# Last product of a SwiGLU feed-forward part and its layer norm: features on the partitions, or tokens

## The reference

```python
D_FF = -(-8 * D_MODEL // (3 * 256)) * 256      # 2816
def layer_norm(x, g, b):
    mu = jnp.mean(xf, axis=-1, keepdims=True)
    var = jnp.mean(jnp.square(xf - mu), axis=-1, keepdims=True)
    y = (xf - mu) * lax.rsqrt(var + LN_EPS)
    return (y * g.astype(jnp.float32) + b.astype(jnp.float32)).astype(x.dtype)
...
x = layer_norm(alpha * x + mix, ln1_g[l], ln1_b[l])
ff = swiglu_ffn(x, w_ffn_gate[l], w_ffn_up[l], w_ffn_down[l])   # (silu(x Wg) * (x Wu)) Wd
x = layer_norm(alpha * x + ff, ln2_g[l], ln2_b[l])
```

## Time and profile before

| | |
|---|---|
| median of 3 runs | 955.96 us (953.98 to 956.77) |
| the profiled execution's own time | 955.32 us |
| its span, first to last instruction | 953.5 us |
| TensorE busy | 889.1 us, 93% |
| VectorE busy | 626.1 us, 66% |
| ScalarE busy | 430.0 us, 45% |
| mean granted TensorE clock | 0.974 |
| DMA over the span | mean 142 GB/s |

### The profile page before, as it was taken

One profiled execution on the slowest core, in us unless ns is written; L12 is line 12 of the kernel. 1 busy time (PEld: TensorE's weight loads), 2 busy tenths in 40 slices (PEclk: granted clock), 3 DMA queues, 4 the chain that ended last, 5 costly groups with the idle time before them and its releaser, 6 DMA issues.

```text
span 953.5 us, 14351 instructions
## 1 busy us (share of the span) xinstructions
PE 889.1 (93%) x5858; PEld 743.8 (78%) x5858; DVE 626.1 (66%) x1242; ACT 430.0 (45%) x721; POOL 0.2 (0%) x4
## 2 busy tenths in 40 slices
PE   4899999999997999999999999898998899999994
PEld 1567468766686958667988888888887899999993
DVE  4442848565657489466699989875685755555554
ACT  3252426444533463455444444564644644444432
POOL 0000000000000000000000000000000000000000
PEclk9899999999997999999999999899999999999998
DMA  9674542101222312433665555331544355557531
GB/s 346 248 287 171 199 177 78 44 2 53 81 89 60 123 60 74 177 102 132 210 198 172 194 177 177 113 100 54 177 129 136 125 184 179 177 161 216 169 98 44
DMA packets 40722, 135.71 MB, mean 142 GB/s; under 512 B 4432, under 2 KB 5584, under 8 KB 40528
## 3 DMA queue, kind: packets, MB, share of 16 engines
q1 hardware_dynamic: 39792, 130.48, 40.8%
q10 hardware_dynamic: 864, 4.32, 1.2%
HBM read 133.73 MB, written 1.05 MB: 141 GB/s over the span
## 4 chain that ended last, share of the span: by engine, by line
PE 81%; DVE 12%; ACT 4%; DMA 1%; issue 1%; SPq 0%; ACTq 0%; DVEq 0%
PE ps L359 12%; PE ps L360 12%; PE ps L364 10%; PE ps L429 3%; PE ps L431 3%; PE ps L430 3%; PE ps L461 3%; PE ps L697 2%; DVE wlo L1384 2%; PE ps L387 2%; PE ps L720 2%; PE ps L606 2%; PE ps L362 2%; DVE AF L1855 1%; PE ps L388 1%; PE ps L389 1%
## 5 line engine op out<-in xcount | busy, mean ns | idle before, releaser
L359 PE MATMUL ps<-hh,whi 128*128 128x256 f32 (+1 forms) x912 | 267.4, 293 | 3.7 <-DVE AF L1900 2.6
L1384 DVE TENSOR_TENSOR wlo<-raw,whi 128x1024 fp32r<-128x1024 f32 (+3 forms) x206 | 233.8, 1149 | 52.8 <-ACT whi L932 52.7
L360 PE MATMUL ps<-hl,whi 128*128 128x256 f32 (+1 forms) x912 | 263.7, 289 | 0.0
L932 ACT ACTIVATE whi<-raw 128x1024 fp32r<-128x1024 f32 (+3 forms) x206 | 204.5, 997 | 128.3 <-DMA raw<-wpack 49.1
L364 PE MATMUL ps<-hh,wlo 128*128 128x256 f32 (+1 forms) x792 | 229.1, 289 | 0.0
L359 PEld LDWEIGHTS ps<-hh,whi 128*128 128x128 f32 x912 | 176.2, 193 | 9.1 <-issue 5.3
L360 PEld LDWEIGHTS ps<-hl,whi 128*128 128x128 f32 x912 | 176.4, 193 | 2.3 <-issue 0.7
L364 PEld LDWEIGHTS ps<-hh,wlo 128*128 128x128 f32 x792 | 153.3, 194 | 1.4
L429 PE MATMUL ps<-whi,hh 128*128 128x512 f32 (+1 forms) x192 | 70.8, 369 | 0.8 <-ACT wk L1035 0.8
L430 PE MATMUL ps<-wlo,hh 128*128 128x512 f32 (+1 forms) x192 | 70.2, 366 | 0.0
L431 PE MATMUL ps<-whi,hl 128*128 128x512 f32 (+1 forms) x192 | 70.2, 366 | 0.0
(11 more groups left out here) (254 smaller groups left out, 1456.3 us busy)
## 6 DMA issues: line engine op xcount, KB each, us to landing
raw<-wpack SPq DMA_DIRECT2D x172, 512.0 KB, 4.1
AF<-wmod SPq DMA_DIRECT2D x40, 512.0 KB, 6.1
raw<-wpack SPq DMA_DIRECT2D x16, 448.0 KB, 3.9
raw<-wpack SPq DMA_DIRECT2D x24, 256.0 KB, 3.3
XT<-xin SPq DMA_DIRECT2D x4, 512.0 KB, 6.7
raw<-wpack SPq DMA_DIRECT2D x4, 432.0 KB, 5.2
uq<-wuq ACTq DMA_DIRECT2D x2, 768.0 KB, 5.7
cst<-cpack ACTq DMA_DIRECT2D x1, 1093.0 KB, 7.9
```

The source lines that it names most:

```text
L359: e.matmul(o, wh[:, b], xh(k), start=j == 0, stop=False, skip_group_check=True)
L360: e.matmul(o, wh[:, b], xl(k), start=False, stop=False, skip_group_check=True)
L932: e.activation(W.hi(i), W.raw(i), ACT.Copy).then_inc(*HI.up(j))
L1384: e.tensor_tensor(W.lo(i), W.raw(i), W.hi(i), ALU.subtract).then_inc(*LO.up(j))
```

## The change

The down product now has the 128 tokens of one tile t as its output partitions and 1024 output features along the free axis, in two PSUM banks for each t, so four banks are held from f = 0 to f = 21. Its stationary operand is a 128 by 128 block of fh or fl, its moving operand 512 columns of a row block of w_down, and one chunk of weights is the whole row block f (128 by 1024). For one f and one t there are six matmuls (three products by two halves of the features). The down step of f - 3 stands behind the gate and up products of f, for f up to 20. The last four f (18 to 21, from `LAST`) stand at the end, first all four for tokens 0 to 127, then all four for tokens 128 to 255; their chunks are given back after the second pass.

In the first four turns four transposes each bring x (the residual) to tokens on the partitions, and ScalarE scales them by alpha into x3t. The norm is done for one tile of tokens at a time on the free axis: one VectorE instruction adds PSUM and x3t and sums the row; ScalarE squares with bias minus mean and sums; VectorE multiplies by gain in the meantime, makes the root on 128 by 1 elements, and writes the result in two halves of 512 columns. SyncE writes four pieces of 256 KB. Gain and bias of the last norm arrive as rows repeated on all partitions, 1 MB, in a DMA that ScalarE issues behind the weights of w_o.

```diff
+LAST = KF - 4
...
+    def down(f, ts):
+
+        if 0 in ts:
+            down_w[f] = weights(("fd", f), ("w_ffn_down_2", 0, (f,), (0, D)), D)
+        c, wh, wl = down_w[f]
+        pe.wait_ge(V["f", f])
+        for t in ts:
+            if f == 0:
+                pe.wait_ge(*ps.take(("fd", t), 2, hold=True))
+            x = slice(t * P, (t + 1) * P)
+            for y, w in ((K.fh, wh), (K.fh, wl), (K.fl, wh)):
+                for q in range(2):
+                    i = e.matmul(ps.ap(("fd", t), 512, 512 * q), y[:, f % 8, x], w[:, 512 * q:512 * q + 512], ...)
+            i.then_inc(*M.up(("fd", f, t)))
+        if 1 in ts:
+            W.given[c] = M.now()
...
-        for m in range(KD):
-            lin(("fd", f0, m), "w_ffn_down_2", 0, (P * m, P), range(f0, f0 + nf), lambda k: K.fh[:, k - f0, :], lambda k: K.fl[:, k - f0, :], 256, lambda k: V["f", k])
-    ln_sums("ln2")
+        if f < 4:
+            t, q = f // 2, f % 2
+            pe.wait_ge(A["x3", 4 * q + 3], *ps.take(("x3t", f)))
+            for j in range(4):
+                i = e.transpose(ps.ap(("x3t", f), P, j * P), K.XT[:, 4 * q + j, 256 + t * P:384 + t * P], C("ident"))
+            i.then_inc(*M.up(("x3t", f)))
+        if 3 <= f < LAST + 3:
+            down(f - 3, (0, 1))
+    for t in range(2):
+        for f in range(LAST, KF):
+            down(f, (t,))
...
+    e.dma_start(K.AF[:, 3072:5120], K.l2rows).then_inc(*K.l2_in.up("rows"))
...
-            ac.wait_ge(V["fu", m], M["fd", f0 - PARTS[0][1] if f0 == 8 else 8, 7] if f0 else None)
+        ac.wait_ge(V["fu", m], M["fd", m - 8, 1] if m >= 8 else None)
...
+        if m < 4:
+            t, q = m // 2, m % 2
+            ac.wait_ge(M["x3t", m])
+            e.activation(g.x3t[:, t, 512 * q:512 * q + 512], ps.ap(("x3t", m)), ACT.Copy, scale=ALPHA).then_inc(*A.up(("x3t", m)))
...
+    for t in range(2):
+        ac.wait_ge(V["lnm", t])
+        e.activation(K.AF[:, 9216:10240], g.x3t[:, t, :], ACT.Square, bias=K.nrm[:, 6 * t:6 * t + 1], accum_out=K.nrm[:, 6 * t + 1:6 * t + 2]).then_inc(*A.up(("lnv", t)))
...
+    for t in range(2):
+        nm, v, u, w = (K.nrm[:, 6 * t + i:6 * t + i + 1] for i in (0, 1, 2, 3))
+        x, y = g.x3t[:, t, :], g.yt[:, t, :]
+        dv.wait_ge(M["fd", KF - 1, t], A["x3t", 2 * t + 1])
+        e.tensor_tensor_reduce(x, ps.ap(("fd", t), D), x, 1.0, 0.0, ALU.add, ALU.add, nm).then_inc(*V.up())
+        dv.wait_ge(V.now())
+        e.tensor_scalar(nm, nm, -1.0 / D, None, ALU.mult, ALU.bypass).then_inc(*V.up(("lnm", t)))
+        dv.wait_ge(V.now(), K.l2_in["rows"])
+        e.scalar_tensor_tensor(out=y, in0=x, scalar=nm, in1=g.l2g, op0=ALU.add, op1=ALU.mult).then_inc(*V.up())
+        dv.wait_ge(A["lnv", t])
+        e.tensor_scalar(v, v, 1.0 / D, LN_EPS, ALU.mult, ALU.add).then_inc(*V.up())
+        rsqrt(v, u, w)
+        dv.wait_ge(V.now())
+        for q in range(2):
+            c = slice(512 * q, 512 * q + 512)
+            e.scalar_tensor_tensor(out=y[:, c], in0=y[:, c], scalar=v, in1=g.l2b[:, c], op0=ALU.mult, op1=ALU.add).then_inc(*V.up(("y", t, q)))
...
-    for k in range(KD):
-        sp.wait_ge(K.act["y", k])
-        e.dma_start(outs[:, k, :], K.XT[:, k, XC]).then_inc(*K.s_out.up("out"))
+    for t in range(2):
+        for q in range(2):
+            sp.wait_ge(K.dve["y", t, q])
+            e.dma_start(K.out[t * P:(t + 1) * P, 512 * q:512 * q + 512], K.G[2].yt[:, t, 512 * q:512 * q + 512]).then_inc(*K.s_out.up("out"))
```

More of the change, by code:

```diff
@@ L905, in tensor_program @@
     xt3 = lambda k: V["x3", k]
[L906 to L914, removed]
-        for m in range(KD):
-            lin(("fd", f0, m), "w_ffn_down_2", 0, (P * m, P), range(f0, f0 + nf), lambda k: K.fh[:, k - f0, :], lambda k: K.fl[:, k - f0, :], 256, lambda k: V["f", k])
-    ln_sums("ln2")
+    def down(f, ts):
[9 more added lines that the diff above has]
+                for q in range(2):
+                    i = e.matmul(ps.ap(("fd", t), 512, 512 * q), y[:, f % 8, x], w[:, 512 * q:512 * q + 512], start=f == 0 and y is K.fh and w is wh, stop=f == KF - 1 and y is K.fl, skip_group_check=True)
+            i.then_inc(*M.up(("fd", f, t)))
+        if 1 in ts:
+            W.given[c] = M.now()
+    down_w = {}
+    for f in range(KF):
+        cc = (P * f, P)
+        if f == 0:
+            lin_many([(("up" if w == "w_ffn_up_2" else "fg", f), w, 0, cc, x2h, x2l, 256) for w in ("w_ffn_gate_2", "w_ffn_up_2")], xt3)
+        else:
+            lin(("fg", f), "w_ffn_gate_2", 0, cc, range(KD), x2h, x2l, 256, xt3)
+            lin(("up", f), "w_ffn_up_2", 0, cc, range(KD), x2h, x2l, 256, xt3)
+        if f < 4:
[9 more added lines that the diff above has]
+            down(f, (t,))
 def scalar_program(K, e):
@@ L1353, in scalar_program @@
     x3(KD - 1)
[L1354 to L1361, removed]
-            ac.wait_ge(V["fu", m], M["fd", f0 - PARTS[0][1] if f0 == 8 else 8, 7] if f0 else None)
[L1363 to L1366, removed]
-    for k in range(KD):
-        ac.wait_ge(V["y", k])
-        e.activation(XT[:, k, XC], XT[:, k, XC], ACT.Identity, bias=C("l2b", k, 1)).then_inc(*A.up(("y", k)))
+    for m in range(KF):
+        z = m % 2 * 256
+        highs(("fg", m))
+        ac.wait_ge(M["fg", m], V["fu", m - 2] if m >= 2 else None)
+        e.activation(K.AF[:, z:z + 256], ps.ap(("fg", m), 256), ACT.Silu).then_inc(*A.up(("fg", m)))
+        ps.give(("fg", m), A.now())
+        highs(("up", m))
+        ac.wait_ge(V["fu", m], M["fd", m - 8, 1] if m >= 8 else None)
+        e.activation(K.fh[:, m % 8, :], K.AF[:, 512 + z:768 + z], ACT.Copy).then_inc(*A.up(("f", m)))
+        if m < 4:
+            t, q = m // 2, m % 2
+            ac.wait_ge(M["x3t", m])
+            e.activation(g.x3t[:, t, 512 * q:512 * q + 512], ps.ap(("x3t", m)), ACT.Copy, scale=ALPHA).then_inc(*A.up(("x3t", m)))
+            ps.give(("x3t", m), A.now())
+        if 3 <= m < LAST + 3:
+            highs(("fd", m - 3))
+    highs(("fd", LAST))
+    for t in range(2):
+        ac.wait_ge(V["lnm", t])
+        e.activation(K.AF[:, 9216:10240], g.x3t[:, t, :], ACT.Square, bias=K.nrm[:, 6 * t:6 * t + 1], accum_out=K.nrm[:, 6 * t + 1:6 * t + 2]).then_inc(*A.up(("lnv", t)))
 def vector_program(K, e):
@@ L2018, in vector_program @@
     x3_low(KD - 1)
[L2019 to L2041, removed]
+    for m in range(KF):
+        z = m % 2 * 256
+        lows(("fg", m))
+        lows(("up", m))
+        h = K.AF[:, 512 + z:768 + z]
+        dv.wait_ge(M["up", m], A["fg", m], V["f", m - 2] if m >= 2 else None)
+        e.tensor_tensor(h, K.AF[:, z:z + 256], ps.ap(("up", m), 256), ALU.mult).then_inc(*V.up(("fu", m)))
+        ps.give(("up", m), V.now())
+        dv.wait_ge(A["f", m])
+        e.tensor_tensor(K.fl[:, m % 8, :], h, K.fh[:, m % 8, :], ALU.subtract).then_inc(*V.up(("f", m)))
+        if 3 <= m < LAST + 3:
+            lows(("fd", m - 3))
@@ L2088, in sync_program, with build @@
     chunks(19, len(W.plan))
-    outs = K.out.rearrange("(k p) n -> p k n", p=P)
-    for k in range(KD):
-        sp.wait_ge(K.act["y", k])
-        e.dma_start(outs[:, k, :], K.XT[:, k, XC]).then_inc(*K.s_out.up("out"))
+    for t in range(2):
+        for q in range(2):
+            sp.wait_ge(K.dve["y", t, q])
+            e.dma_start(K.out[t * P:(t + 1) * P, 512 * q:512 * q + 512], K.G[2].yt[:, t, 512 * q:512 * q + 512]).then_inc(*K.s_out.up("out"))
     sp.wait_ge(K.s_out["out"])
-def build(nc, cpack, xin, wpack, wmod, wuq, wukv, out):
+def build(nc, cpack, xin, wpack, wmod, wuq, wukv, l2rows, out):
     with ExitStack() as ctx:
@@ L2104, in sig @@
             return Sig(ctx.enter_context(nc.semaphore(name)), step)
-        K.cpack, K.xin, K.wpack, K.wmod, K.wuq, K.wukv, K.out = cpack, xin, wpack, wmod, wuq, wukv, out
+        K.cpack, K.xin, K.wpack, K.wmod, K.wuq, K.wukv, K.l2rows, K.out = cpack, xin, wpack, wmod, wuq, wukv, l2rows, out
         K.NAF = 22408
@@ L2255 @@
     vi = nc.dram_tensor("wukv", (2, P, 1024), F32, kind="ExternalInput").ap()
-    oo = nc.dram_tensor("out", (D, T), F32, kind="ExternalOutput").ap()
-    plan = build(nc, ci, xi, wi, mi, ui, vi, oo)
+    li = nc.dram_tensor("l2rows", (P, 2 * D), F32, kind="ExternalInput").ap()
+    oo = nc.dram_tensor("out", (T, D), F32, kind="ExternalOutput").ap()
+    plan = build(nc, ci, xi, wi, mi, ui, vi, li, oo)
     def cols(v, n):
```

18 lines of the change are left out of this document (10 added, 8 removed).

## The result

The changed kernel takes 943.14 us, the median of 4 runs (940.30 to 944.47), against 955.02 us for four runs of the kernel before. The ratio is 0.987, with a 95% interval of 0.984 to 0.990. The forecast was 945.6 us, with a range of 943.0 to 949.2. So the direction and the order of the change were right, and the range was set too high: of the nine executions in both sets the median is 942.23, and five lie under 943.0.

What follows compares the result with a forecast made beforehand. TensorE was taken to bound the kernel, with a serial 18.58 us end. Down products -3.5, transposes +1.8 and end -8.7 sum to -10.4 us, from 955.96 to 945.6 us; range 943.0 to 949.2.

Steps and rivals of the forecast that it cites:

- What bounds the kernel: Whole kernel: TensorE has 81% of the chain; worth costing are matmul start distance and the 18.58 us end.
- Down products: Feed-forward down step: 528 matmuls at 0.120 us become 264 of double width at 0.227 us, -3.5 us.
- Rival B: Down products: 512-wide matmuls beside 256-wide ones cost 0.240 us, so they gain nothing; 949.1 us, chance 4%.
- Transposes: Turns of f = 0 to 3: 16 new transposes on TensorE at 0.11 us each, all on the path, +1.8 us.
- Waits in the turns: Feed-forward turns: weight loads, low splits and PSUM banks keep up with TensorE, so no added wait, 0 us.
- Rival A: Down steps: TensorE waits for weights' low splits, up to 27 us more, 972.7 us, slower than before; chance 4%.
- The end: Behind the last down product: norm and output take 9.9 us instead of 18.58, -8.7 us, ends -9.5 and -7.7.
- The output: Last write at the end: 2.83 us for 128 KB plus 0.4 for 128 KB more, 3.2 to 3.3 us.
- Tile 0's hold: At the end: tile 0's chain still holds VectorE 0.5 us when tile 1 is ready.
- The chain itself: VectorE's norm chain for one tile at the end: 1.54 + 1.39 + 1.5 + 1.5 = 5.9 us.
- Rival C: Norm at the end: VectorE steps with two SBUF operands take double, +4.2 us, 949.8 us; chance 4%.

Runs made afterwards that it cites:

- half: The changed kernel with each 512-column down-product matmul issued as two of 256 columns, except the first into each bank: 947.23 us, ratio 0.992 to the kernel before.
- out4: The kernel before with its output written in four pieces of 256 KB instead of eight of 128 KB: span 951.9 us in one execution.
- last3: The changed kernel with three down steps instead of four in the two passes at the end: 9.85 us from last product to span's end, one execution.
- again: The changed kernel unaltered, run once more: median 942.23 us of 5 runs, ratio 0.987 to the kernel before.
- warm: The changed kernel with ten unused float32 matmuls filling TensorE's wait ahead of the first gate product: 942.26 us, ratio 0.986 to the kernel before.
- best: The kernel of warm with five down steps in the passes, tile 1's pass and addition by feature halves, output cut 768 and 256 columns: 942.05 us.
- best2: The kernel of best with the output cut 512 and 512 columns again: 942.37 us, ratio 0.987 to the kernel before.

## Why the prediction came out as it did

**What bounds the kernel**: right. The gain lay in the two places that the views pointed to, TensorE's start distance and the serial end.

**Down products, -3.5**: right in mechanism, 0.4 too large. The run half gives -3.1, because each step of wide matmuls costs 0.03 us more than twelve times 0.227. Rival B (0) is out. The Trainium skill's spacing of N/2.4 + 2.5 ns ("TensorE: Matmul & The Clock Gate", section "Back-to-back issue gap") would have given 0.7 us; the run half measures 3.1. The section calls this the gap of an isolated matmul, which the prediction left out, and gives about 131 ns for 512 columns in a stream of weight loads and matmuls. The trace agrees with neither: for these matmuls, each with its own weight load, starts are 120 ns apart at 256 columns (formula 109) and 227 at 512 (formula 216).

**Transposes, +1.8**: right. 1.7 from the trace, 1.77 by doubling them.

**Waits in the turns, 0**: right. Rival A had its place and its price but no wait appeared. The load rates in that paragraph are 5% too low: with 1024 bytes to the KB they are 193 against 182 GB/s, and nothing hung on it.

**The end, -8.7**: this is the term that failed. It measured -10.1, 1.4 more, and beyond its own low bound of -9.5. Three parts were priced too high, by 0.9, 0.3 and 0.2 us:
- The output. "3.2 to 3.3" measured 2.43. The step was to take 2.83 us from the last activation to the end as the price of a 128 KB write and add 0.4 for its size. The run out4 shows that 0.6 of it was the backlog of eight writes, which four pieces don't have. The 0.4 for the size came from loads (4.1 us for 512 KB, 3.3 for 256); from the last issue on the larger write took only 0.2 to 0.3 more (2.41 and 2.5 for 2.24). Both numbers of the backlog were in the earlier trace rows: the issues run from 947.90 for 3.81 us, to 951.71, while the activations end at 950.67.
- Tile 0's hold. "0.5" measured 0.16, because the chain takes 5.6 and not 5.9 us (924.78 to 930.38, when the next addition starts). last3 confirms how it grows.
- The chain itself. 5.69 for 5.9: the addition with its small steps took 1.45 for 1.54, the square and its handover 1.28 for 1.39, the two halves 1.42 for 1.5.

**Rival C** is out: the gain step took 1.28 us, not 2.36. The Trainium skill's remark that such a step "halves throughput" ("Vector Engine (DVE) Microarchitecture Reference", section "7. Points that are easy to get wrong") has no counterpart in this trace.

**The sum and the range.** With the measured terms, -3.1 + 1.8 - 10.1 = -11.4 instead of -10.4, the same sum gives 944.6 us, which is inside the range. So the end alone did not carry the result to 942.23. Another 0.9 us is the base: the forecast subtracts from 955.96, the median of three runs, and nine runs of the kernel before, taken with again, have a median of 955.10. The last 1.5 us (0.9 by the ratio) no trace accounts for, and they are less than the uncertainty of about 2. Below 945.6 the range had 0.8 us for the end and some 1.8 for the medians, 2.6 in all; the measured terms took 1.0, base and rest 2.4, all in one direction. The upper half of the range, up to B's 949.2, was never near.

## What to carry to other kernels

When the price of a last write is read from a trace, measure it from the start of its issue, and look whether the issues before it ran behind the engine that feeds them; here 128 KB writes that became ready 0.41 us apart left 0.50 us apart. Where an end works on two tiles, let the matmul order make the first ready one chain's length ahead of the second, counted in matmuls. A norm along the free axis, at the end of a kernel, trades matmuls with ones and full-width passes for one-column operations of 0.16 us.

## What the runs showed of the hardware

The same matmuls ahead of the first gate product ended between 738.6 and 744.4 us in seven traces of the changed kernel and its variants (743.44 and 742.01 in two of the kernel before and its variant), so one profiled execution against one other can mislead by over 5 us, more than three times the 1.4 us by which the end was mis-sized. Up to 3.3 us of that is how long the clock stood at 0.50. Comparing stretches from landmark to landmark brought the spread down to 0.02 us for traces with the same half-clock time at the start (S of 190.05 and 190.07 with 3.1 us, 191.43 and 191.42 with 6.1).

After a wait of 5.3 us TensorE ran at half clock (granted 0.50) for 3.1 or 6.1 us, with matmuls of 256 columns 0.213 us apart, in different executions of the same kernel. With the wait filled by other matmuls it was at full clock in all three traces (warm, best, best2). Against these the half clock cost 0.2 us in the first case, 1.6 in the second, and 0.5 where it lasted 3.6 (last3). From 3.6 to 6.1 us that is 0.44 us for each us: at 0.213 us a matmul instead of 0.120 it costs in full, once the stops for the normed tiles are used up.
